# First four jobs of a two-block kernel taken in turn over pairs of input tiles, with the weight stream, the early splits and the convolution's taps laid out anew

## What is computed

```python
h = rms_norm(x, norm1_g)                 # x / sqrt(mean(x*x) + eps) * g
z = h @ w_in                             # columns: glu_in (2 x 1024), q, k, v, gate_logits
a_val, a_gate = jnp.split(glu_in, 2, axis=-1)
a = a_val * jax.nn.sigmoid(a_gate)
a = causal_depthwise_conv(a, conv_w, conv_b)   # 31 taps per channel
a = jax.nn.silu(rms_norm(a, conv_norm_g))
y_a = a @ w_conv_out
```

## Time and profile before

| | |
|---|---|
| median of 3 runs | 829.39 us (828.84 to 829.65) |
| profiled execution, its own time | 830.8 us |
| its span, from the first to the last instruction | 829.0 us |
| PE busy | 818.0 us, 99% of the span |
| DVE busy | 649.4 us, 78% |
| ACT busy | 554.0 us, 67% |
| POOL busy | 228.6 us, 28% |
| mean granted clock of PE | 0.999 of full speed |

### The profile page before, as it was taken

How to read it: one execution, slowest core, us unless ns; L and a number is a source line. 1 busy time by engine, 2 the same in 40 slices (tenths; PEclk the granted TensorE clock), 3 DMA queues, 4 the chain that set the end, 5 groups by cost and what they waited for, 6 DMA issues and landing times.

```text
span 829.0 us, 16592 instructions
## 1 busy us (share of the span) xinstructions
PE 818.0 (99%) x6010; PEld 764.2 (92%) x6010; DVE 649.4 (78%) x1172; ACT 554.0 (67%) x1022; POOL 228.6 (28%) x245
## 2 busy tenths in 40 slices
PE   8999999999999999999999999999999999999996
PEld 8998998999999999999889989999998988888886
DVE  7998989997979998787766978756689866666552
ACT  8777999996756776666555776386647665655442
POOL 0387852332312244333101000020022333322110
PEclk9999999999999999999999999999999999999999
DMA  7666654546565376555646445435446566665741
GB/s 271 218 197 194 179 172 141 160 141 197 155 200 185 129 224 201 186 181 176 229 159 222 153 157 176 132 124 179 127 144 193 178 209 193 182 199 165 234 135 51
DMA packets 43168, 146.12 MB, mean 176 GB/s; under 512 B 4928, under 2 KB 7632, under 8 KB 43088
## 3 DMA queue, kind: packets, MB, share of 16 engines
q1 hardware_dynamic: 42192, 144.13, 55.0%
q10 hardware_dynamic: 896, 0.94, 0.4%
HBM read 144.00 MB, written 1.05 MB: 175 GB/s over the span
## 4 chain that ended last, share of the span: by engine, by line
PE 89%; DVE 5%; ACT 4%; issue 2%; DMA 1%; SPq 0%; DVEq 0%; ACTq 0%
PE px L561 20%; PE px L565 17%; PE px L567 16%; PE px L566 16%; PE px L562 10%; DVE wlo L1466 2%; PE px L571 1%; PE px L573 1%; PE px L572 1%; PE px L638 1%; PE px L787 1%; ACT whi L941 1%; DVE hx L1734 1%; PE px L650 1%; DMA raw<-ws 1%
## 5 line engine op out<-in xcount | busy, mean ns | idle before, releaser
L1466 DVE TENSOR_TENSOR wlo<-raw,whi 128x1024 fp32r<-128x1024 f32 x265 | 331.2, 1256 | 26.7 <-ACT whi L941 26.6
L941 ACT ACTIVATE whi<-raw 128x1024 fp32r<-128x1024 f32 x265 | 278.1, 1052 | 53.6 <-PE px L562 25.8
L565 PE MATMUL px<-hx,whi 128*128 128x256 f32 x1024 | 293.7, 287 | 0.9 <-DVE hx L1483 0.3
L566 PE MATMUL px<-hx,whi 128*128 128x256 f32 x1024 | 286.5, 280 | 0.0
L567 PE MATMUL px<-hx,wlo 128*128 128x256 f32 x1024 | 285.7, 279 | 0.0
L565 PEld LDWEIGHTS px<-hx,whi 128*128 128x128 f32 x1024 | 192.6, 188 | 4.5 <-issue 1.6
L566 PEld LDWEIGHTS px<-hx,whi 128*128 128x128 f32 x1024 | 192.9, 188 | 0.5
L567 PEld LDWEIGHTS px<-hx,wlo 128*128 128x128 f32 x1024 | 192.8, 188 | 0.0
L2119 POOL TENSOR_TENSOR CA<-CA,ct 128x256 f32<-128x256 f32 x90 | 89.9, 999 | 97.5 <-DVE wlo L1466 72.5
L561 PE MATMUL px<-fx,whi 128*128 128x512 f32 x330 | 114.5, 391 | 0.0
L561 PE MATMUL px<-hx,whi 128*128 128x512 f32 x320 | 111.1, 391 | 0.0
(11 more groups left out here) (331 smaller groups left out, 1319.1 us busy)
## 6 DMA issues: line engine op xcount, KB each, us to landing
raw<-ws SPq DMA_DIRECT2D x265, 512.0 KB, 3.6
tb<-tabs SPq DMA_DIRECT2D x16, 128.0 KB, 3.5
X<-xs SPq DMA_DIRECT2D x4, 256.0 KB, 4.0
raw<-ws SPq DMA_DIRECT2D x3, 256.0 KB, 5.7
out<-Y SPq DMA_DIRECT2D x1, 384.0 KB, 2.4
vc<-vecs SPq DMA_DIRECT2D x1, 315.5 KB, 7.0
raw<-ws ACTq DMA_DIRECT2D x1, 256.0 KB, 4.1
msk<-lmask ACTq DMA_DIRECT2D x1, 256.0 KB, 2.9
```

The costliest lines, as they stand in the source:

```text
L565: e.matmul(b[:, 0:S], H, xh, start=first, stop=False)
L566: e.matmul(b[:, 0:S], H, xl, start=False, stop=False)
L941: e.activation(whi[:, n % NSL, :], raw[:, n % NRAW, :], ACT.Copy).then_inc(s_hi, 1)
L1466: e.tensor_tensor(wlo[:, n % NSL, :], raw[:, n % NRAW, :], whi[:, n % NSL, :], ALU.subtract).then_inc(s_lo, 1)
```

## The change

The first four jobs ag0, av0, ag1, av1 are no longer run one after the other. PE takes tiles 0 and 1 of all four, then tiles 2 and 3 of all four, and so on. The stream is laid out to match: chunk p holds the blocks of tiles 2p and 2p + 1 of the four jobs. Chunks 0 to 3 come in pieces (`PIECES`: two quarters and a half of chunk 0, then halves), split between the `ax` tiles. The sums stand behind all four jobs instead of two. `EARLY` is 4, so eight jobs use `ax`, and ag4 is the first on `hx`. `WARM` is 8. The first half chunk is issued by SP, not ACT, and x and weights alternate on SP's queue. The program of DVE and ACT between 1 / rms and ag4 is written anew, and the taps are dealt out by other quotas, from chunk 8 instead of 6.

```diff
-HALVED = 2
-WARM = 16
-EARLY = 3
+HALVED = 4
+PIECES = [(0, 0, 256), (0, 256, 512), (0, 512, CW)] + [(c, h, h + CW // 2) for c in range(1, HALVED) for h in (0, CW // 2)]
+WARM = 8
+EARLY = 4
+FOUR = [("ag", 0), ("av", 0), ("ag", 1), ("av", 1)]
...
+def spot(key, k, kt, at, w):
+    if key in FOUR:
+        return k // 2 * CB + 2 * FOUR.index(key) + k % 2
+    return at + k * w
...
-        quota = (2.2 if c < 12 else 3.2 if c < 24 else 2.6 if c < 34 else 3.7, 2.0 if c < 34 else 1.8)
+        quota = (2.9 if c < 12 else 3.2 if c < 24 else 3.0 if c < 34 else 3.6, 2.1 if c < 24 else 1.7 if c < 44 else 2.2)
...
-            for i in range(EARLY):
-                job(("ag", i), AX, first_scaled if i == 0 else None, rings=(FEW,))
+            for k in range(0, KD, 2):
+                for key in FOUR:
+                    job(key, AX, first_scaled if key == FOUR[0] else None, rings=(FEW if key[0] == "ag" else SMALL,),
+                        tiles=(k, k + 1))
+            sums("n1", VALUES)
+            for i in range(2, EARLY):
+                job(("ag", i), AX, rings=(FEW,))
                 job(("av", i), AX, rings=(SMALL,))
-                if i == 0:
-                    sums("n1", VALUES)
...
-            highs(3)
+                for piece in PIECES_AT[i]:
+                    piece_high(*piece)
+                if i == 5:
+                    e.activation(sqa[:, :, :], X[:, 0:2, :], ACT.Square).then_inc(s_sq, 1)
+                elif i > 5:
+                    e.activation(sq[:, 2 * i - 12:2 * i - 10, :], X[:, 2 * i - 10:2 * i - 8, :], ACT.Square).then_inc(s_sq, 1)
+            piece_high(*PIECES[-1])
+            e.activation(sq[:, 4:6, :], X[:, 6:8, :], ACT.Square).then_inc(s_sq, 1)
+            highs(5)
             rms("n1", D)
...
             for i in range(3):
+                if i == 2:
+                    piece_low(*PIECES[-1])
                 e.wait_ge(s_sq, i + 2)
...
-            lows(3)
+            lows(5)
...
+            lows(9)
+            early(("av", 2), CI[:, 2, 30:])
+            early_gated(2)
             e.wait_ge(s_vc, 16)
...
-            early(("av", 2), CI[:, 2, 30:])
-            early_gated(2)
+            e.wait_ge(s_ci, 1)
+            early(("ag", 3), sg[:, 0, :])
+            early(("av", 3), CI[:, 3, 30:])
+            early_gated(3)
...
             tiles(0)
+            half_load(0, 0)
+            half_load(0, 1)
             tiles(1)
+            half_load(1, 0)
             tiles(2)
+            half_load(1, 1)
             tiles(3)
-            half_load(0, 1)
-            half_load(1, 0)
-            half_load(1, 1)
-            loads(2)
+            half_load(2, 0)
+            half_load(2, 1)
+            half_load(3, 0)
+            half_load(3, 1)
+            loads(5)
```

More of the change, by code:

```diff
@@ L138, with block_order @@
 BEHIND = (("uv", 1), ("ckv", 0), ("fu", 1))
+def spot(key, k, kt, at, w):
+    if key in FOUR:
+        return k // 2 * CB + 2 * FOUR.index(key) + k % 2
+    return at + k * w
+def block_order(placed):
+    for pair in range(KD // 2):
+        for key in FOUR:
+            for k in (2 * pair, 2 * pair + 1):
+                yield key, k
+    for key, _, _, kt, _ in placed[len(FOUR):]:
+        for k in range(kt):
+            yield key, k
 def milestones():
@@ L148, in milestones @@
         where[key] = (kt, at, w)
-        for k in range(kt):
-            final[(at + k * w) // CB] = (key, k)
+    order = [(key, k, spot(key, k, *where[key]) // CB) for key, k in block_order(placed)]
+    for key, k, c in order:
+        final[c] = (key, k)
     n, ends, used, blocks = 0, {}, {}, {}
[L152 to L160, removed]
+    for key, k, c in order:
+        end = k == where[key][0] - 1
+        if final[c] == (key, k) or end or key in BEHIND:
+            n += 1
+            blocks[key, k] = n
+            if final[c] == (key, k):
+                used[c] = n
+            if end:
+                ends[key] = n
     return where, ends, used, blocks
@@ L461, in two_blocks @@
         FROM = norm_counts()
-        LOW = {c: (s_lo, c + 1 + min(c + 1, HALVED)) for c in range(n_chunks)}
-        HI = [c + 1 + min(c + 1, HALVED) for c in range(n_chunks)]
+        PIECE = {p: n + 1 for n, p in enumerate(PIECES)}
+        HI = [PIECE[c, CW // 2, CW] if c < HALVED else len(PIECES) + c + 1 - HALVED for c in range(n_chunks)]
+        LOW = {c: (s_lo, HI[c]) for c in range(n_chunks)}
         def half(h):
@@ L539, in take, with job @@
                 return px[b]
-            def job(key, xs, ready=None, rings=None):
+            def job(key, xs, ready=None, rings=None, tiles=None):
                 kt, at_, w = WHERE[key]
                 rings = rings or (JOBS, JOBS)
-                banks = [take((key, t), rings[t]) for t in range(1 if w == 1 else 2)]
-                for k in range(kt):
+                tiles = tiles or range(kt)
+                if tiles[0] == 0:
+                    banks = [take((key, t), rings[t]) for t in range(1 if w == 1 else 2)]
+                else:
+                    banks = [px_of[key, t] for t in range(1 if w == 1 else 2)]
+                for k in tiles:
                     if ready:
                         ready(k)
-                    c, o = (at_ + k * w) // CB, (at_ + k * w) % CB * P
-                    if c < HALVED and o in (0, CW // 2):
-                        e.wait_ge(s_lo, 2 * c + 1 + (o > 0))
+                    b = spot(key, k, kt, at_, w)
+                    c, o = b // CB, b % CB * P
+                    if c < HALVED:
+                        for piece in PIECES:
+                            if piece[:2] == (c, o):
+                                e.wait_ge(s_lo, PIECE[piece])
                     elif c >= HALVED and c != seen[0]:
@@ L927, in _, with piece_high @@
             made = [HALVED]
-            def half_high(n, h):
-                e.wait_ge(s_raw[n] if h else s_half[n], 16)
-                e.activation(whi[:, n, half(h)], raw[:, n, half(h)], ACT.Copy).then_inc(s_hi, 1)
+            def piece_high(n, a, b):
+                e.wait_ge(s_half[n] if a < CW // 2 else s_raw[n], 16)
+                e.activation(whi[:, n, a:b], raw[:, n, a:b], ACT.Copy).then_inc(s_hi, 1)
             def highs(c):
@@ L1002, in early_gate @@
                 e.wait_ge(*BANK[("ag", i), 0])
-                e.activation(sg[:, i, :], sg[:, i, :], ACT.Tanh, scale=0.5).then_inc(s_eg, 1)
+                e.activation(sg[:, i % 3, :], sg[:, i % 3, :], ACT.Tanh, scale=0.5).then_inc(s_eg, 1)
             def first_high(i):
@@ L1007, in first_high @@
                 e.activation(hx[:, i, 0, :], sq[:, nt_slot("n1", i), :], ACT.Copy).then_inc(s_nhi, 1)
-            highs(4)
-            for i in range(2):
+            highs(6)
+            for i in range(3):
                 first_high(i)
             early_gate(0)
-            first_high(2)
-            highs(5)
-            for i in (3, 4):
+            early_gate(1)
+            highs(7)
+            for i in range(3, 6):
                 first_high(i)
[L1017 to L1020, removed]
+            highs(9)
             for i in (6, 7):
@@ L1023, in _ @@
             early_gate(2)
+            early_gate(3)
             def products(c):
@@ L1452, in _, with piece_low @@
             made = [HALVED]
-            def half_low(n, h):
-                e.wait_ge(s_hi, 2 * n + h + 1)
-                e.tensor_tensor(wlo[:, n, half(h)], raw[:, n, half(h)], whi[:, n, half(h)], ALU.subtract).then_inc(s_lo, 1)
+            def piece_low(n, a, b):
+                e.wait_ge(s_hi, PIECE[n, a, b])
+                e.tensor_tensor(wlo[:, n, a:b], raw[:, n, a:b], whi[:, n, a:b], ALU.subtract).then_inc(s_lo, 1)
             def lows(c):
@@ L1506, in _ @@
                                        op0=ALU.mult, op1=ALU.subtract).then_inc(s_xgl, 1)
[L1507 to L1512, removed]
+                for piece in PIECES_AT[i]:
+                    piece_low(*piece)
             for i in range(3):
+                if i == 2:
+                    piece_low(*PIECES[-1])
                 e.wait_ge(s_sq, i + 2)
@@ L1527, in early_gated @@
                 e.wait_ge(*BANK[("av", i), 0])
-                e.scalar_tensor_tensor(out=CI[:, i, 30:], in0=sg[:, i, :], scalar=1.0, in1=CI[:, i, 30:], op0=ALU.add,
+                e.scalar_tensor_tensor(out=CI[:, i, 30:], in0=sg[:, i % 3, :], scalar=1.0, in1=CI[:, i, 30:], op0=ALU.add,
                                        op1=ALU.mult).then_inc(s_ci, 1)
@@ L1537, in _ @@
             e.wait_ge(s_rms, 1)
+            first_tiles((0, 1, 2), ())
             early(("ag", 0), sg[:, 0, :])
+            early(("ag", 1), sg[:, 1, :])
+            first_tiles((), (0, 1, 2))
+            lows(6)
+            first_tiles((3, 4, 5), ())
             early(("av", 0), CI[:, 0, 30:])
[L1540 to L1543, removed]
+            early(("av", 1), CI[:, 1, 30:])
+            lows(7)
             early_gated(0)
[L1545 to L1548, removed]
             early_gated(1)
```

(13 more changed lines are left out.)

3 lines of the change are left out of this document (2 added, 1 removed).

## The result

The changed kernel takes 833.13 us (median of 5 runs, 832.58 to 834.62) against 829.65 (828.84 to 829.96, 5 runs) beside it: a ratio of 1.0046 [1.0035, 1.0057], **3.5 us slower** where 829.5 us, no change, was forecast. Its profiled execution took 832.82 us, span 831.0.

A forecast was written before the change was run, and what follows sets the result against it. The prediction took PE to bound the kernel, busy 818.01 of 829.00 us; +0.4 at ag5 (1.5 us won at the start, paid back) and -0.3 for the taps gave +0.1, from 829.39 to 829.5 us, range 828.4 to 830.6.

The forecast's parts named there:

- The start: First four jobs and sums: first job at 5.7 us, jobs' end at 18.0, ag2 at 18.9; 1.5 us won.
- The ag5 stage: From 1 / rms to ag5: waits of 0.4 us at av4, 1.5 at ag5; ag5 at 37.8 us, 0.4 later.
- The taps: Chunks 24 to 54, taps and products dealt out anew on DVE and ACT: -0.3 us, from -0.6 to +1.5.
- the attention wait: PE's 0.6 us wait for an ACT copy near 143 us: about 0.3 us of it was to go.
- The third: New PE wait in the tap stages from ACT's 22 products or DVE's 30 taps: 2 us, 831.5; chance 0.06.
- The second: PE's clock still low in the first jobs, ten slow blocks: +2 us, 831.5; chance 0.1.
- The first: DVE keeps up to ag5, so the 1.5 us won stay: 827.6 us, or 827.1; chance 0.22.

The follow-up runs named there:

- the order experiment: Changed kernel with chunk 10's high part ahead of ag3's tanh on ACT and DVE's work for ag3 earlier: 831.84 us, 1.0017 of before.
- the quota experiment: Kernel with all three edits, GpSimd's quota now 2.0 up to chunk 33, 1.6 to 42 and 2.3 after: 829.64 us, 0.9992 of before.
- the one before with the turned ring: Kernel before the change, with one step less in the turn of the three-bank ring ahead of the ao jobs: 830.68 us, 1.0007 of before.
- the ring phase: Changed kernel with one step more in the turn of PE's three-bank ring ahead of the ao jobs: 832.78 us, 1.0031 of before.
- the taps: Changed kernel with a flat quota of 2.0 GpSimd taps for each chunk: 832.23 us, 1.0027 of before.
- all three edits: Changed kernel with the ring turned one step more, the flat quota of 2.0 and the new order on ACT and DVE: 829.85 us, 0.9994 of before.
- the last piece: As the quota experiment, with DVE's low part of chunk 3's last half ahead of its second addition of squares: 829.56 us, 0.9991 of before.

## Why the prediction was wrong

**The start** was right. First job at 5.39 (forecast 5.7), the four jobs' end at 18.2 (18.0), ag2 behind the sums at 18.89 (18.9), so 1.5 us won (1.5), or 1.3 by its second matmul. From the first job to the sums the forecast had 12.3 us for 11.3 us of blocks, 1.0 of waiting without a place; measured are 12.8, with waits of 1 us at 9.24 and 0.4 at 16.70. A first job 0.3 us earlier and waits 0.5 us longer cancel to 0.2, and that part of the agreement is luck.

**The ag5 stage** was right, and in its order too. 1 / rms at 20.31 (20.06), 0.46 us at av4 (0.4), 1.40 at ag5 (1.5), ACT standing 3.10 us for DVE's `early` ahead of its tanh, DVE 0.52 us for ACT's high part; ag5 at 37.95 (37.8), which is 17.64 us behind 1 / rms (17.7). Counting DVE's program from single rows and asking what ACT's in-order queue holds ahead of the high part gave this to 0.1 us, and the order experiment shows the cause: with the split of chunk 10 ahead of the tanh on ACT, and DVE's steps for ag3 and chunk 10 earlier, both waits are gone.

**The taps are the step that failed**: "-0.3 us, from -0.6 to +1.5". It named the attention wait rightly (0.56 for 0.78, so -0.2), and missed the head sum (+1.3) and the small ones at 173 and 181 (+0.3), +1.4 in all. That lies just inside the term's own bounds, but what those allowed for was a DVE or ACT near full. (A slip in its count: DVE has 28 taps in chunks 34 to 41, not as many as before, 30.) I had compared loads: ACT's and DVE's taps for a stretch against their idle time there. From that view 17 products for 20 looks like relief. The wait falls on ACT, which is not full there: ACT's second product for a new tile can't start before POOL's last sum of the old one, and where that stands in ACT's queue is decided by the plan. DVE is the full one, and POOL nearly so, as the busy times of PE, its weight loads, DVE, ACT and POOL up to the end of POOL's tile show:

```profile
64.20:81.55 17.35, 17.35 (x94) 14.81 (x93) 17.35 (x32) 10.46 (x17) 15.50 (x13) 1.00 0.74 215
```

POOL had no term in the prediction at all.

It should have had one. POOL's sum of 128x256 takes 0.74 us in the median of the 57 sums of the trace after that overlap a `wlo` subtraction of DVE by less than 0.05 us, and 1.34 us, up to 1.78, in the 33 that overlap one for longer; the duration grows with the overlap (correlation 0.93 here, 0.94 before), and does not grow with that with DVE's other instructions (-0.10, 0.02). The Trainium skill (SBUF — State Buffer, "Who interferes with whom") says that a DVE instruction with two inputs in SBUF contends with a GpSimd instruction that reads SBUF, because they share a read interface. Both traces agree, though no experiment took the overlap away. So where DVE splits a chunk each 2.8 us, POOL's chain of sums is slower than a count of 0.74 each says, and it is POOL's end that the v copies waited for.

**The ring was left out,** a second step that failed. No term, no rival: `EARLY` from 3 to 4 changes how often a bank ring is turned, and 180 us later a job gets the bank of its predecessor: +0.8 us, shown from both sides. Another 0.2 us at 199.6 is the last attention heads' `ax` on DVE, as in the quota experiment but smaller.

Sum at places: +0.6 at ag5 (forecast +0.4), -0.1, +1.3, -0.2, +0.4, +1.0, which is +3.0, and by the trace +3.1 us behind ao2, against +0.1 forecast.

**The rivals.** The third (a new wait in the tap stages, 831.5) is nearest to what came, but its reason, ACT's 22 products or DVE's 30 taps, is not what the trace shows for the big one. The second (low clock) is not what happened in the trace after, where matmuls start every 0.117 us from 5.4 us on. Its condition does occur, as one trace with the same eight `ones` shows (slow up to 9.2 us), but its price of 2 us is refuted: without any `ones` seven slow blocks cost 0.3 us, since most of it falls into gaps. The first (DVE keeps up) is what the order experiment makes true. The waits at av4 and ag5, 1.9 us, go, and 1.3 us of it are left behind ao2.

## What to carry to other kernels

When an edit shifts a plan, don't compare loads only: list for each in-order engine which instruction waits for a slower helper at each hand-over (here a tile's end on POOL), and what is queued behind it. Any count that feeds a ring of buffers (jobs, splits, turns) has a phase; when it changes by one, check every place where two rings share a buffer, however far behind. A gain at the start can be lost at places that have nothing to do with the start: here three later waits, each with a cause of its own, took more than it had given.

## What was not expected of the hardware

**Pace.** Between 290 and 390 us a block takes some 0.354 us in some traces and 0.351 in others. Busy time, instructions and clock in about the same hundred us of work, of before and then of after:

```profile
289.00:390.00 101.00, 101.00 (x855) 100.80 (x855) 86.04 (x132) 66.79 (x112) 40.84 (x38) 1.00 0.64 196
```

```profile
291.00:392.00 101.00, 101.00 (x863) 100.80 (x863) 86.86 (x133) 67.93 (x113) 42.34 (x38) 1.00 0.65 198
```

PE never pauses in either, the clock column says 1.00 in both, and one gets through 8 matmuls more. Matmul by matmul there are two paces and nothing between: the changed kernel, the one before with the turned ring, and the ones with the ring phase, the taps, all three edits and the last piece gain 0.96 or 0.97 us on before in this stretch; those with the order, the last quotas and no `ones` gain 0.02 at most. This is why the difference of +3.1 us at 204 shrinks to +2.0 between the two profiled executions, while the medians differ by 3.5. So one profile's span can be 1 us off for this alone. The gaps repeat better from trace to trace: 1.39 to 1.40 at ag5, 0.72 to 0.73 at ao2, 1.1 to 1.3 at the head sum. With one trace of each kernel, whether the pace belongs to the kernel or to the execution is open, and so is what sets it.

**The clock column** reads 1.00 also over the first seven blocks of the kernel without `ones`, which run at half pace. The trace's record of the clock has its first entry, of full speed, at 9.77 us, just where the spacing changes, and the column counts the time ahead of it as full. In the first 10 us the spacing of matmuls says what the clock is, and the column does not.
